# Moving the weight-half sums of a seven-product matmul stage from GpSimd to VectorE, with a second set of modulation rows on TensorE and a column-strip router product

## The reference, cut to what matters

```python
sh1, sc1, g1, sh2, sc2, g2 = adaln(silu_c, ada_w[layer], ada_b[layer])
a = modulate(rmsnorm(h, norm1_w[layer]), sh1, sc1)
u = a @ w_in                     # layer 0: 768 x 1024 by 1024 x 5680, float32
conv_in, z, v, o, dt, ig, fg = split(u)
...                              # conv, SSD scan, mLSTM scan
h = h + g1 * (y @ w_out)
t = modulate(rmsnorm(h, norm2_w[layer]), sh2, sc2)
p_group = softmax(t @ w_group); e_logits = t @ w_expert   # 4 + 16 columns
```

## Time and profile before

| | |
|---|---|
| Median of 3 runs | 1678.41 us (1675.86 to 1678.69) |
| Profiled execution: its time | 1679.96 us |
| Profiled execution: its span, first to last instruction | 1678.2 us |
| Mean granted TensorE clock | 0.940 |
| PE busy | 1481.8 us, 88% |
| DVE busy | 941.0 us, 56% |
| ACT busy | 462.1 us, 28% |
| POOL busy | 363.2 us, 22% |

### The profile page before, as it was taken

The page is one execution under the profiler, slowest core; times in us unless marked ns, Lnnn a source line. Parts: engine busy times, 40 slices in busy tenths (PEclk is TensorE's granted clock), DMA queues, the critical chain, the costliest instruction groups (busy, mean ns, idle before and its releaser), DMA issues. The chain is left out here.

```text
span 1678.2 us, 19694 instructions
## 1 busy us (share of the span) xinstructions
PE 1481.8 (88%) x7462; PEld 862.3 (51%) x7462; DVE 941.0 (56%) x1467; ACT 462.1 (28%) x946; POOL 363.2 (22%) x295
## 2 busy tenths in 40 slices
PE   4999999999997999799995999759978999959895
PEld 2555558787776777544553343324434554433341
DVE  4669989898883667355425211134546663463125
ACT  4132113000006677422211111124215663110001
POOL 1232334333323685412100100011000000001001
PEclk8999999999997999899996999979988999979998
DMA  9546655656666999653424899664004002758994
GB/s 345 180 151 207 226 182 199 238 213 238 213 217 197 306 284 256 250 187 114 160 90 192 320 397 418 258 224 177 13 9 94 2 0 84 305 201 337 420 396 163
DMA packets 166175, 355.07 MB, mean 212 GB/s; under 512 B 17041, under 2 KB 107489, under 8 KB 147265
## 3 DMA queue, kind: packets, MB, share of 16 engines
q1 hardware_dynamic: 144520, 278.31, 47.8%
q0 software_dynamic: 16288, 58.12, 9.1%
q10 hardware_dynamic: 5273, 17.38, 2.6%
HBM read 297.72 MB, written 56.05 MB: 211 GB/s over the span
## 5 line engine op out<-in xcount | busy, mean ns | idle before, releaser
L2608 PE MATMUL ex_ps_gu<-room,ex_xT 128*32 128x512 f32 x1472 | 169.8, 612 | 10.3 <-DMA room<-in_moe_w_up_dram 5.2
L2026 PE MATMUL po_ps_y<-room,po_yT 128*128 128x512 f32 x320 | 140.8, 598 | 2.0 <-DVE po_n L1925 2.0
L698 PE MATMUL ie_pq<-room,aT_even 128*128 128x256 f32 x576 | 130.2, 384 | 2.0 <-POOL room L842 2.0
L698 PEld LDWEIGHTS ie_pq<-room,aT_even 128*128 128x128 f32 x576 | 110.6, 193 | 21.1 <-issue 3.3
L2608 PEld LDWEIGHTS ex_ps_gu<-room,ex_xT 128*32 128x32 f32 x1472 | 56.8, 113 | 115.6 <-issue 110.4
L694 PE MATMUL ie_pq<-aT_even,room 128*128 128x384 f32 x320 | 108.3, 486 | 0.0
L2759 DVE TENSOR_TENSOR ex_hid<-ex_hid,ex_ps_gu 128x256 f32<-128x256 f32 x25 | 10.5, 422 | 163.8 <-ACT ex_hid L2706 163.8
L2026 PEld LDWEIGHTS po_ps_y<-room,po_yT 128*128 128x128 f32 x320 | 60.6, 192 | 75.1 <-issue 72.9
L2633 PE MATMUL ex_ps_d<-room,ex_hT 128*32 128x512 f32 x736 | 83.7, 594 | 4.7 <-DVE ex_hT L2763 3.2
L1111 DVE SCALAR_TENSOR_TENSOR room<-room,ccol 128x2048 f32<-128x2048 f32 x28 | 82.3, 2940 | 0.0
L1111 DVE SCALAR_TENSOR_TENSOR xzo<-room,ccol,xzo 128x2048 f32<-128x2048 f32 x28 | 79.8, 2852 | 0.0
(11 more groups left out here) (535 smaller groups left out, 2709.6 us busy)
## 6 DMA issues: line engine op xcount, KB each, us to landing
room<-in_ada_w_dram SPq DMA_DIRECT2D x37, 1024.0 KB, 5.1
room<-in_moe_w_gate_dram SPq DMA_DIRECT2D x33, 1024.0 KB, 11.7
room<-in_moe_w_up_dram SPq DMA_DIRECT2D x33, 1024.0 KB, 14.3
room<-in_moe_w_down_dram SPq DMA_DIRECT2D x33, 1024.0 KB, 13.7
room<-in_ev_w_in_dram SPq DMA_DIRECT2D x6, 2048.0 KB, 12.6
room<-ac_rows SPq DMA_DIRECT2D x12, 1024.0 KB, 6.5
y<-ex_y ACTq DMA_DIRECT2D x24, 512.0 KB, 8.4
room<-in_ev_w_in_dram SPq DMA_DIRECT2D x10, 1024.0 KB, 6.0
```

The source lines that it names most:

```text
L698: ins = nc.tensor.matmul(to[:, T * 2 * P:(T + 1) * 2 * P], x[:, k, T * P:(T + 1) * P], w[:, k, :], start=(k == 0), stop=(k == KH - 1))
L2026: last = nc.tensor.matmul(ps_y[:, c * BANK:(c + 1) * BANK], yT[n % 2][:, k, :] if even else kit.oT[:, k, n * P:(n + 1) * P], (w[:, k] if e ...
L2608: last = MM(ps_gu[s][rows, :, :], xT[s][:, k, rows], wgu[slot[q]][:, :, k, :], start=(k == 0), stop=(k == KD - 1))
```

## The change

- All four weight-half sums move from GpSimd's queue to VectorE's. In a conv pair the order on VectorE becomes `c12, taps, s1, u2, taps, s3(q+1), u3, to_tokens, c21, gates step, c11, s4, s2(q+1), to_tokens, c22_u4`. GpSimd keeps the stores.
- A second adaLN unit goes to TensorE (`DIRECT` = 2). Each of the conv pairs 2 to 9 now does two direct slots, one after p7 and one after p2. Each slot's weights come as four DMAs of 512 columns instead of one of 2048. The second unit's weights lie in four tiles that are idle then, among them the second half of `mixed_w`. VectorE weighs 24 slots instead of 32, four in each z block, and there are three `sum_ada` instead of four, two of them after p5.
- The conv pairs' PSUM ring shrinks from five banks to four, to make room for the second accumulator.
- The wait for the stores of the modulation rows moves out of this phase into the recurrent phase's SyncE queue, ahead of the second set of row loads.
- The router product is done on strips: the folded router weights, padded to 32 columns, are stationary and the 128 tokens move, with four blocks of the contraction side by side in four column strips (two rounds). ScalarE copies the strips out, and one more matmul folds them into 128x20. `take_logits` moves later on VectorE.
- GpSimd clears the semaphores of layer 0's `phase_out` at the end of layer 0's experts.

```diff
-    ADA_SLOTS = (len(ADA_ORDER) - 1) * KD
+    DIRECT = 2
+    ADA_SLOTS = (len(ADA_ORDER) - DIRECT) * KD
...
-        RING, ZRING = (0, 1, 2, 3, 6), 3
+        RING, ZRING = 4, (2, 4, 0)
...
+        def s4(eng, q):
+            a11, a12, a21, a22, s2 = weights(q)
+            eng.wait_ge(s2_ready, q + 1)
+
+            eng.wait_ge(p2_done, q + 1)
+            return a12, a12, s2, ALU.subtract
...
+                for v in range(DIRECT):
+                    if q > 2:
+
+                        sp.wait_ge(direct_read[v], q - 2)
+                    elif v:
+                        sp.wait_ge(tail_ready, 1)
+                    rows = ada_rows(v, q - 2)
+                    for j in range(4):
+                        sp.dma_start(direct_w[v][j], rows[:, j * BANK:(j + 1) * BANK]).then_inc(direct_loaded[v], 16)
...
-            Z_AT = {5: 2, 11: 3, 16: 4, 22: 5}
+            Z_AT = {4: 2, 8: 3, 12: 4, 16: 5}
...
-            sp.wait_ge(mod_stored, 128)
...
-            SUMS = {(PAIRS + 1, 3, 0): 1, (PAIRS + 2, 6, 0): 2, (PAIRS + 4, 2, 0): 3, (LAST, 5, 0): 4}
+            SUMS = {(PAIRS + 1, 5, 2): 2, (PAIRS + 3, 5, 2): 3, (LAST, 5, 0): 4}
...
                 p7(q)
+                if 2 <= q < PAIRS:
+                    direct(q - 2, 0)
                 p4(q)
...
                 if 2 <= q < PAIRS:
-                    direct(q - 2)
+                    direct(q - 2, 1)
                 p5(q)
...
                     taps(q - 1, 0)
+                TT(*s1(dve, q)).then_inc(s1_ready, 1)
                 u2(q)
                 if q:
                     taps(q - 1, 1)
+                TT(*s3(dve, q + 1)).then_inc(s3_ready, 1)
                 u3(q)
...
                 if q:
                     next(steps)
                 c11(q)
+                TT(*s4(dve, q)).then_inc(s4_ready, 1)
+                if q == PAIRS - 1:
+                    dve.wait_ge(direct_read[1], KD)
+                TT(*s2(dve, q + 1)).then_inc(s2_ready, 1)
...
-                for k in range(KD):
-                    last = nc.tensor.matmul(ps_r[:, 0:20], tT[:, k, :], wrs[s][:, k, :], start=(k == 0), stop=(k == KD - 1))
-                last.then_inc(logits_done, 1)
+                for k in range(KD):
+                    j = k % 4
+                    last = nc.tensor.matmul(ps_s[32 * j:32 * j + 32, 0:P], wrs[s][:, k, :], tT[:, k, :], start=(k < 4), stop=(k >= 4))
+                last.then_inc(strips_done, 1)
+
+            def fold_logits(n):
+                pe.wait_ge(strips_out, n + 1)
+                if n:
+
+                    pe.wait_ge(logits_out, n)
+                nc.tensor.matmul(ps_r[:, 0:20], strips, fold, start=True, stop=True).then_inc(logits_done, 1)
```

More of the change, by code:

```diff
@@ L407, in phase_in_even @@
         mixed_w = sb("mixed_w", [P, KH * 2 * P])
+        direct_w = [[late[:, j * BANK:(j + 1) * BANK] for j in range(4)],
+                    [kit.tokS[:, :, :].rearrange("p t c -> p (t c)")[:, 0:BANK], kit.tokM[:, :, :].rearrange("p t c -> p (t c)")[:, 0:BANK],
+                     w_tail[:, :, :].rearrange("p k n -> p (k n)")[:, 0:BANK], mixed_w[:, KH * P:KH * 2 * P]]]
         pq = st.enter_context(nc.psum_tensor("ie_pq", [P, 8 * BANK], F32))
@@ L748, in turn, with direct @@
                 last.then_inc(turned, 1)
-            def direct(k):
-                pe.wait_ge(direct_loaded, 16 * (k + 1))
-                ada_slot(nc, ada_acc, kit.ccol, k, direct_w).then_inc(direct_read, 1)
+            def direct(k, v):
+                pe.wait_ge(direct_loaded[v], 64 * (k + 1))
+                for j in range(4):
+                    last = nc.tensor.matmul(direct_acc[v][32 * j:32 * j + 32, :], kit.ccol[:, k, :], direct_w[v][j], start=(k == 0), stop=(k == KD - 1))
+                last.then_inc(direct_read[v], 1)
             def sum_ada(v):
-                pe.wait_ge(ada_step, 2 * KD * v)
-                if v == 1:
+                pe.wait_ge(ada_step, 2 * KD * (v - DIRECT + 1))
+                if v == DIRECT:
                     pe.wait_ge(keep_clear, 2)
@@ L1151, in _ @@
                     taps(q - 1, 1)
[L1152 to L1157, removed]
+                some(1)
+                TT(*s1(dve, q)).then_inc(s1_ready, 1)
+                some(1)
                 u2(q)
+                if q < LAST:
+                    TT(*s3(dve, q + 1)).then_inc(s3_ready, 1)
                 some(1)
                 u3(q)
-                some(1)
-                if q == PAIRS + 3:
-                    take_row(2)
[L1164 to L1169, removed]
+                if q == PAIRS + 1:
+                    take_row(0)
+                    take_row(1)
+                c21(q)
+                if q == PAIRS + 1:
+                    next(steps)
+                some(1)
+                c11(q)
+                TT(*s4(dve, q)).then_inc(s4_ready, 1)
+                if q < LAST:
+                    TT(*s2(dve, q + 1)).then_inc(s2_ready, 1)
+                if q == PAIRS + 2:
+                    take_row(2)
                 if q == PAIRS + 4:
                     take_row(3)
-                c11(q)
                 if q == LAST:
                     take_row(4)
-                else:
-                    some(1)
                 c22_u4(q)
@@ L1873, in _ @@
                     take_t(n - 2)
+                if even and n > 2:
+                    take_strips(n - 2)
                 if even and n + 1 < count:
@@ L1877, in _ @@
                     prepare(n + 2)
+                if even and n == 2:
+                    take_strips(0)
                 if n and (not even or n + 1 == count):
                     take_t(n - 1)
+                    take_strips(n - 1)
                 square(n)
@@ L1883, in _ @@
                 root(n)
+            take_strips(count - 1)
         @block.vector
@@ L1985, in _ @@
                     take_shift()
-                if even and n >= 3:
+                if not even and n >= 2:
                     take_logits(n - 2)
@@ L1992, in _ @@
                 gates(n, 1)
+                if even and n >= 3:
+                    take_logits(n - 2)
+                if not even and n == 0:
+                    fold_router()
+                norm(n)
                 if even and n == 2:
@@ L1995, in _ @@
                 if n + 1 == count:
-                    take_logits(n - 1)
-                if not even and n == 0:
-                    fold_router()
-                norm(n)
-                if not even and 0 < n < count - 1:
                     take_logits(n - 1)
```

139 lines of the change are left out of this document (75 added, 64 removed).

## The result

The changed kernel takes 1667.38 us, the median of 4 runs (1664.08 to 1673.08); the kernel before took 1678.55 (4 runs, 1675.86 to 1680.27). The ratio is 0.993, with a 95% interval from 0.9901 to 0.9959: faster by 11 us, 0.7%. The forecast was 1674 in a range from 1662 to 1684, with 0.48 on faster.

A forecast was written before the change was run, and what follows sets the result against it. VectorE's adaLN work set PE's time in the z blocks; PE nearly set its own in the conv pairs. Conv pairs +20.4, clock +6.0, z blocks -25.5, phase end -2.5, router -3.0: -4.6, so 1674 us, range 1662 to 1684.

The forecast's parts named there:

- the forecast (A): Whole kernel: the z blocks' gain is given back in the conv pairs; 1668 to 1680 us, chance 0.52.
- Z blocks: Z blocks: sums off GpSimd shorten VectorE's slots to 4.6 us, PE waits vanish; 250.83 to 225.3 us, a gain of 25.5.
- Rival D: Z blocks: moving the sums does not free VectorE, slots stay 5.8 us, gain only 18; kernel 1681 us, chance 0.13.
- Conv pairs at full clock: Conv pairs: 209.0 us without stalls plus 16.9 of p3 waiting for s4; 225.9 us, 20.4 more than before.
- the 0.3 for the release of PE: Conv pairs: about 0.3 us assumed after s4 to release PE and load its weights before p3.
- The four steps beside GpSimd: Conv pairs 1, 5, 6, 8: gates steps with an operation doubled beside GpSimd shrink by about 1.0, 1.1, 0.9, 0.8 us.
- The clock: Conv pairs: low clock after the three new stalls of 3.5 us or longer, 2 us each; 6.0 us lost.
- End of the stage: Stage end: moving the wait for the modulation rows' stores gains 2.5 us, between 0 and 3.
- the row of GpSimd's 3.00: Stage end: GpSimd stood 3.00 us at the phase's end, from 513.0 to 516.0.
- Router: Router products on strips: 0.7 us saved each, six counted, less about 1.2 of waits; net 3.0 us gained.
- Rival B: Conv pairs: s4 is in time, 209 to 213 us, clock untouched; kernel near 1651, with milder forms chance 0.15.
- Rival C: Conv pairs: five stalls cost 13.5 us of low clock, gates steps do not shrink; kernel 1685 us, chance 0.20.

The follow-up runs named there:

- run 4: The changed kernel with all weight-half sums, of conv pairs and z blocks, back on GpSimd, both adaLN units still on TensorE; 1655.15 us, ratio 0.986.
- run 2: The changed kernel with the gates step behind the token copy, and in pairs 3, 4, 6 and 8 cut in two, the first part ahead of c11; 1648.21 us.
- run 7: The kernel before with one edit: on GpSimd s2 of the next pair goes ahead of the token store; 1677.55 us, ratio 0.9993.
- run 6: The changed kernel with the conv pairs' sums back on GpSimd and s2 issued ahead of the token store; 1647.17 us, again 1645.2.
- run 9: The kernel before with only the wait for the stores of the modulation rows moved to the next phase; 1676.53 us, ratio 0.9987.
- run 3: The changed kernel with the four sums of each conv pair back on GpSimd, z blocks' sums still on VectorE; 1653.93 us, ratio 0.9851.
- run 8: As run 6 but with one direct adaLN unit, the ring of five banks, single loads and the four sums of before; 1648.72 us, ratio 0.9819.
- run 1: The changed kernel with each conv pair's gates step moved behind c11, s4, s2 and the token copy; 1660.43 us, ratio 0.9904.
- run 5: The kernel before, one direct unit, with only the z blocks' sums moved to VectorE; 1666.14 us, ratio 0.9918.
- run 10: The kernel before with only the router products on strips with a fold, in both layers; 1673.7 us, ratio 0.9972.

## Why the prediction was right, and where it was off

The mechanism of the forecast (A) is what happened: the gain of the z blocks is given back in the conv pairs, by p3 waiting for s4 behind the gates step. The measured 1667.38 us lies 0.6 below the likeliest case's own range (1668 to 1680) and inside the whole one. The two large terms were right to a microsecond each; that the total came out clearly faster is in part luck, since the terms that I can measure give only 6.6 of the 11 us (last point).

- **Z blocks.** 225.3 predicted, 224.81 measured, with no wait and the clock at 1.00. Sums on VectorE were 0.69 and 1.22 us as read off the slope. The reason that I gave was only part of it: I explained the lost 33 us by slots stretched beside GpSimd. That is real (run 4), but the second unit with the new places of the sums, which I had costed in the conv pairs and hardly credited in the z blocks, would have given 24.6 alone (table above). Rival D, slots that stay long, would therefore have cost 1.5 us and not 7 or 8: its mechanism was priced against a VectorE load with the old number of slots.
- **Conv pairs at full clock.** 225.9 predicted; 231.37 less 6.5 of low clock is 224.9. The stalls by pair (1, 3, 4, 5, 6, 8) were 0.6, 3.3, 4.0, 1.4, 2.0 and 4.4 against 0.8, 3.5, 4.2, 1.6, 2.2 and 4.6: 0.2 less in each. (They are counted from where p3 could have started; the table of waits, whose ends are modelled, has 14.6 in all.) The term that was too large is the 0.3 for the release of PE: in pair 4 s4 ends at 163.79 and p3 starts at 163.85. The four steps beside GpSimd shrank as expected: in pairs 1, 5, 6 and 8 from 4.84, 7.62, 8.01 and 10.29 to 3.86, 6.52, 7.12 and 9.45. Without any stall I had 209.0; run 2 takes 210.01 with 0.7 of waits; the 199.4 in it were 0.5 too low (199.88 busy in run 7). The direct slots cost 9.4 in place of 9.6 (PE is busy for 209.30 us in run 6 and for 199.88 in run 7).
- **The clock.** 6.0 predicted, 6.5 measured: 1.8, 1.8 and 2.9 behind the waits of 3.3, 4.0 and 4.4 us, nothing behind the shorter ones but the 0.1 of every wait. The Trainium skill (TensorE: Matmul & The Clock Gate, "HAM oscillation") says that gaps drop the array to half clock. By that rule the three long stalls had to cost something, and the trace agrees with these three losses. It also has three stalls, of 0.6, 1.4 and 2.0 us, that cost no clock, and the waits of 2.65 us below show that the length of a gap alone doesn't settle it.
- **End of the stage.** 2.5 predicted, 3.3 measured (3.6 in run 9): the row of GpSimd's 3.00 was the better bound.
- **Router.** 3.0 predicted, 3.1 measured, 2.0 in the even layer and 1.1 in the odd one. A product saved 1.0 and not 0.7 (16 records in 0.58, a fold of 0.14), so the net is right while its parts are not: that is luck.
- **The size.** My sum was -4.6; the same terms measured in the profile are +25.85 - 26.02 - 3.3 - 3.1 = -6.6. The medians say -11.2 (-6.9 to -16.6). The 4.6 us between are not explained. They are not all scatter of the changed kernel: with the windows of their own profiles the medians of runs 2, 3, 4, 6 and 8, which have the same small parts, lie 2.2 to 3.1 us below the same sum (4.9 when run 6 was measured again), and only that of run 1 lies above it, by 1.8. So some 2 to 3 us may be gained outside the stretches that I measured; what it is stays open. One profiled execution of each kernel was compared, that of the changed kernel 5.7 above its median; its late start (1.75) and the clock of the output phase (1.8) show by how much single places differ from one execution to the next. In the next forecast I would take the profiled execution's scatter into the range.

Rival B (s4 in time, near 1651) describes the kernel of run 2 and not this one: VectorE did have the room, but the order was fixed, as the argument against it said. Rival C (1685) needed a low clock after all five stalls; it followed three.

## What to carry to other kernels

When a duty moves to an in-order queue, look for the longest block ahead of it there and for the deadline behind it: the same sums on the same engine cost 21 us behind a 9 us step and nothing once that step was cut in two and partly moved back. Price two edits that relieve the same engine as a table of four, since the second of them is worth little: here 15.7 and 24.6 gave 26.0 together. And a wait that is removed ahead of a stretch which another engine bounds can be worth nothing: run 7 saved 5.4 us in the conv pairs and lost them in the z blocks, where PE waited for VectorE. The same edit was worth 6.5 us (216.67 to 210.12) as soon as that bound was gone (run 6).

## What the runs showed of the hardware

The same wait, for s2 in conv pair 9, is followed by the full clock or by the low one. It was 2.66 us in the kernel before and in run 5, and 2.65 in runs 3, 4, 9 and 10. Windows over the product behind it, of before and of run 3 (here to the start of the next product):

```profile
242.31:244.99 2.68, 2.68 (x8) 1.62 (x9) 2.61 (x3) 0.56 (x2) 2.66 (x2) 1.00 0.61 205
```
```profile
251.16:255.51 4.35, 4.35 (x9) 2.44 (x9) 4.28 (x4) 0.56 (x2) 4.09 (x2) 0.61 0.37 127
```

Run 5 repeats the first case, runs 4, 9 and 10 the second (4.33, 4.37 and 3.94 us), and runs 9 and 10 have the code of before in this stage. In the conv pairs of these traces waits of up to 2.0 us never cost any clock, waits of 3.1 to 4.3 always did, and the one of 2.65 did in four of six kernels. In the z blocks a wait of 2.05 us for GpSimd's s4 was followed by 0.51 in the kernel before (eight records took 3.68 us) and by 1.00 in runs 7, 9 and 10 (1.99 to 2.00 us). The output phase's first 16 us show the same: 0.89 in three of the thirteen profiles and 1.00 in the other ten, with the same work around it, worth 1.8 us, and more than most of the small terms of this change.

VectorE's 2048-column operation takes 2.34 us alone and up to 4.44 beside a sum of GpSimd; eight tap operations took 4.81 in one kernel and 8.77 in another, where they lay beside GpSimd's 128x1024 sums. Two cases in the z blocks of run 4 show that it matters which starts first: a slot's instruction that started at 279.10, inside a sum of GpSimd from 278.06, took 4.44 us and the sum 3.33; one that started at 295.28, 0.14 ahead of a sum, took 2.34 and the sum 4.43. On strips a record of 32 weight columns with 128 moving columns took 36 ns on average (0.58 for 16), a third of the 106 of the old router product.
